# Halo x loads taken at a lower rate in the placement estimate, their work placed with more slack, and a last output tile left whole, in a hybrid attention and pooling layer

## The reference

```python
h = rms_norm(x, norm_gain)
proj = einsum('bsd,de->bse', h, w_in)      # 2048 -> 16384 columns
q, k, v, z_attn, u_pool, z_pool, gates = split(proj)
# A: three dilated sliding windows (128,1) (512,4) (2048,16), 8 heads each, mixed by softmax denominators
y_attn = (attn * silu(z_attn)) @ w_branch_attn
# B: trailing means over 2, 4, 8, 16 positions minus the token, 256 channels each
pool = concat(d_g @ pool_maps[g]) * pool_scale
y_pool = (pool * silu(z_pool)) @ w_branch_pool
g_attn, g_pool = split(sigmoid(gates + b_gates))
out = x + (g_attn * y_attn + g_pool * y_pool) @ w_out
```

## Time and profile before

| | |
|---|---|
| median of 3 runs | 1585.2 us |
| the profiled run | 1585.16 us, span of its slowest core (core 4) 1583.4 us |
| spans of the cores 0 to 7 | 1579.7, 1579.3, 1581.5, 1577.0, 1583.4, 1577.5, 1580.2, 1579.9 us |
| core 4: TensorE busy | 1545.1 us, 98% of the span |
| core 4: VectorE, ScalarE busy | 639.8 us (40%), 602.3 us (38%) |
| core 4, 80 to 120 us: TensorE busy, granted clock, DMA share | 35.60 of 40 us, 0.91, 0.97 |
| core 4, 120 to 160 us | 38.98 of 40 us, 1.00, 0.89 |
| core 4, 160 to 200 us | 38.72 of 40 us, 1.00, 0.43 |
| core 4, 200 to 1500 us | 1298.1 of 1300 us, 1.00 |

### The profile page before, as it was taken

How to read it: one execution, slowest core, us unless ns; L and a number is a source line. 1 busy time by engine, 2 the same in 40 slices (tenths; PEclk the granted TensorE clock), 3 DMA queues, 4 the chain that set the end, 5 groups by cost and what they waited for, 6 DMA issues and landing times.

```text
span 1583.4 us, 27047 instructions; the slowest of 8 cores (1577.0 to 1583.4 us)
## 1 busy us (share of the span) xinstructions
PE 1545.1 (98%) x10216; PEld 935.8 (59%) x10216; DVE 639.8 (40%) x840; ACT 602.3 (38%) x985; POOL 86.9 (5%) x168
## 2 busy tenths in 40 slices
PE   5889999999999999999999999999999999999997
PEld 4655668656864756849656964856544444444443
DVE  5777723165415445543164515354522211113211
ACT  3667535353435543455353435553631111110000
POOL 0000000000000000000000000000000101000000
PEclk8999999999999999999999999999999999999999
DMA  9798441123131143231123131243545556542983
GB/s 241 186 246 216 90 84 33 27 52 73 31 54 34 35 78 68 48 68 32 35 54 64 32 54 34 50 72 63 120 81 92 97 105 107 89 73 39 207 218 107
DMA packets 43073, 138.04 MB, mean 87 GB/s; under 512 B 7041, under 2 KB 8321, under 8 KB 39681
## 3 DMA queue, kind: packets, MB, share of 16 engines
q0 software_dynamic: 23552, 85.58, 32.1%
q1 hardware_dynamic: 14640, 42.29, 8.4%
q10 hardware_dynamic: 4754, 8.45, 1.9%
HBM read 206.86 MB, written 10.49 MB: 137 GB/s over the span
## 4 chain that ended last, share of the span: by engine, by line
PE 90%; DMA 4%; DVE 2%; ACT 2%; issue 1%; SPq 0%; DVEq 0%; ACTq 0%
PE p_pp L464 74%; PE p_pnd L464 6%; PE p_psc L464 5%; PE p_pS L464 3%; DMA s_xt<-xh 3%; DMA pt_spill<-s_pt 1%; DVE s_ub L475 1%; ACT s_xn L545 1%; PE p_pnd L568 1%; ACT s_rr L468 1%; DVE s_xn L479 0%; DMA s_rot<-s_qS 0%; DMA s_rot<-s_kS 0%; ACT s_jk L545 0%; DVE s_kS L475 0%
## 5 line engine op out<-in xcount | busy, mean ns | idle before, releaser
L464 PE MATMUL p_pp<-s_hTo,s_wr 128*128 128x512 bf16 (+4 forms) x3616 | 765.1, 365 | 10.4 <-DMA s_wr<-w_in 4.4
L464 PEld LDWEIGHTS p_pp<-s_hTo,s_wr 128*128 128x128 bf16 x3616 | 343.1, 99 | 368.0 <-issue 16.2
L479 DVE SCALAR_TENSOR_TENSOR s_kS<-p_pp,s_cst,s_rr 128x512 bf16<-128x512 f32 (+1 forms) x96 | 94.6, 986 | 271.1 <-ACT s_rr L468 236.6
L464 PE MATMUL p_pp<-s_wr,s_hTo 128*128 128x256 bf16 x1536 | 175.4, 273 | 1.4 <-DVE s_qS L479 1.4
L464 PEld LDWEIGHTS p_pp<-s_wr,s_hTo 128*128 128x128 bf16 x1536 | 160.7, 119 | 8.0 <-issue 1.7
L464 PE MATMUL p_pp<-s_wr,s_hTh 128*128 128x256 bf16 x1344 | 159.5, 273 | 0.0
L464 PE MATMUL p_pp<-s_hTh,s_wr 128*128 128x512 bf16 (+1 forms) x768 | 155.2, 352 | 0.0
L468 ACT ACTIVATE s_rr<-p_pS 128x512 f32<-128x512 f32 x144 | 83.6, 580 | 181.8 <-PE p_pS L464 172.9
L464 PEld LDWEIGHTS p_pp<-s_wr,s_hTh 128*128 128x128 bf16 x1344 | 145.3, 137 | 1.9
L468 ACT ACTIVATE s_rr<-s_rr 128x512 f32<-128x512 f32 x208 | 128.5, 618 | 19.7 <-ACT s_rr L468 1.1
L487 POOL DMA_DIRECT2D s_wr<-w_in x128 | 67.7, 529 | 1212.1 <-PE p_pp L464 760.9
(11 more groups left out here) (75 smaller groups left out, 1203.8 us busy)
## 6 DMA issues: line engine op xcount, KB each, us to landing
s_wr<-w_in POOLq DMA_DIRECT2D x128, 512.0 KB, 5.1
s_xt<-xh SPq DMA_DIRECT2D x23, 1024.0 KB, 9.4
s_wr<-w_y POOLq DMA_DIRECT2D x16, 512.0 KB, 4.9
s_wo<-w_out POOLq DMA_DIRECT2D x16, 512.0 KB, 7.4
s_xr<-xh ACTq DMA_DIRECT2D x32, 256.0 KB, 7.5
out<-s_ob SPq DMA_DIRECT2D x31, 256.0 KB, 6.0
pt_spill<-s_pt SPq DMA_DIRECT2D x8, 256.0 KB, 6.5
s_pT<-pt_spill SPq DMA_DIRECT2D x1, 2048.0 KB, 12.3
```

The costliest lines, as they stand in the source:

```text
L464: S.op("pe", lambda t: t.matmul(out, lhsT=lhsT, rhs=rhs, start=start, stop=stop), reads=reads, writes=writes, cost=n / 2400.0 + 0.0025)
L479: S.op("dve", lambda v: v.scalar_tensor_tensor(out=out, in0=in0, scalar=scalar, in1=in1, op0=op0, op1=op1), reads=reads, writes=writes, co ...
```

## The change

Three edits. The first: a DMA of 1 MB or more on SyncE's queue is taken to move 180 KB per us in the planner's estimate, where it was 270. The second: the margin of a condition is now its own field, 0.6 us as before except for the two conditions of a halo tile (its Square and scale, and each half of its transposes), where it is 2.5 us. Both act through the planner alone: the same instructions, in other places of the lists. The third: the last of the 32 output tiles, which was done as two halves of 256 columns, each with its own matmuls, addition and DMA, is done like the others.

```diff
         if o.isdma:
             self.T[eng] = at + 0.1
-            self.chan[eng] = max(self.chan[eng], at + 1.5) + kb / (270.0 if kb >= 1024 else 540.0)
+            rate = 180.0 if eng == "sp" else 270.0
+            self.chan[eng] = max(self.chan[eng], at + 1.5) + kb / (rate if kb >= 1024 else 540.0)
             o.end = self.chan[eng] + 0.7
...
     def when(self, t):
         c = t.cond
-        at = self.S.ready_at(c.reads, c.writes) + self.MARGIN
+        at = self.S.ready_at(c.reads, c.writes) + c.margin
         for r in c.rings:
             i = r.ctr % r.n
-            at = max(at, self.S.ready_at((), (r.B[i],)) + self.MARGIN)
+            at = max(at, self.S.ready_at((), (r.B[i],)) + 0.6)
...
-                yield Cond(reads=[xt.B[loaded[j]]], rings=[xn], heavy=XLATE)
+                yield Cond(reads=[xt.B[loaded[j]]], rings=[xn], heavy=XLATE, margin=2.5)
...
-                    yield Cond(reads=[xn.B[slot[j]], B_id], rings=[pnd], heavy=XLATE)
+                    yield Cond(reads=[xn.B[slot[j]], B_id], rings=[pnd], heavy=XLATE, margin=2.5)
...
-                parts = [(0, 512)] if (cg, tt_) != (3, 7) else [(0, 256), (256, 256)]
-                for part, (c0, cn) in enumerate(parts):
-                    if part:
-                        P, BP = banks[n_out % 4]
-                    for db in range(KC):
-                        mm(P[:, c0:c0 + cn], mT[:, db, ts_], wo[cg][:, db, c0:c0 + cn], db == 0, db == KC - 1, cn,
-                           [B_mT[db], B_wo[cg]], [BP])
-                    o_ap = ob_t[oi][:, c0:c0 + cn]
-                    stt(o_ap, P[:, c0:c0 + cn], 0.5, xr_t[xi][:, c0:c0 + cn], ALU.mult, ALU.add, cn, [BP, xr.B[xi]],
-                        [ob.B[oi]])
-                    cs = slice(512 * cg + c0, 512 * cg + c0 + cn)
-                    S.op("sp", lambda s, o_ap=o_ap, ts_=ts_, cs=cs: s.dma_start(out=out_d[ts_, cs], in_=o_ap),
-                         reads=[ob.B[oi]], dsem="dp2" if part else f"do{oi}", kb=cn // 2)
+                for db in range(KC):
+                    mm(P[:], mT[:, db, ts_], wo[cg][:, db, :], db == 0, db == KC - 1, 512, [B_mT[db], B_wo[cg]], [BP])
+                stt(ob_t[oi][:], P[:], 0.5, xr_t[xi][:], ALU.mult, ALU.add, 512, [BP, xr.B[xi]], [ob.B[oi]])
+                S.op("sp", lambda s, oi=oi, ts_=ts_, cs=cs: s.dma_start(out=out_d[ts_, cs], in_=ob_t[oi][:]),
+                     reads=[ob.B[oi]], dsem=f"do{oi}", kb=256)
```

More of the change, by code:

```diff
@@ L207, with __init__ @@
 class Cond:
-    __slots__ = ("reads", "writes", "rings", "after", "heavy")
-    def __init__(self, reads=(), writes=(), rings=(), after=(), heavy=0.0):
+    __slots__ = ("reads", "writes", "rings", "after", "heavy", "margin")
+    def __init__(self, reads=(), writes=(), rings=(), after=(), heavy=0.0, margin=0.6):
         self.heavy = heavy
+        self.margin = margin
         self.reads = reads
@@ L225 @@
 class Tasks:
-    MARGIN = 0.6
     def __init__(self, S):
```

## The result

The changed kernel took 1589.97 us in the median of seven runs, the kernel before 1584.89 in the runs beside them: a ratio of 1.0036 with a 95% interval of 1.0023 to 1.0048, or 3.6 to 7.6 us slower. The profiled run took 1589.7 us. The forecast was 1589.1 us and slower. The spans of the cores 0 to 7 are 1581.5, 1583.3, 1588.1, 1586.4, 1586.3, 1583.7, 1585.2 and 1581.5 us: all are longer than before, by 1.6 to 9.4 us. The slowest core is now core 2; I compare core 4 with itself, and then add what core 2 has more.

What follows compares the result with a forecast made beforehand. TensorE, busy for 98% of the span, was taken as the bound. On 1585.16 us, -7.2 + 3.6 + 5.4 + 0.1 = +1.9 gives 1587.1, and 2.0 for the clock 1589.1 us; range 1584.5 to 1591.5.

Steps and rivals of the forecast that it cites:

- gaps of tiles 13 and 14, half clock: Pooling stage, core 4: TensorE's waits before these tiles' transposes and the half clock behind them go, -7.2 us together.
- tile 9 behind the `s_zs` wait: First group: tile 9's transposes, which ran ahead of the wait at 77.46, now stand behind it, +0.9 us.
- z3's map, z1's bank: First group: z3's map waits for the bank of z1's map, given back behind tile 14's scale, +0.7 us.
- second u group, z3's bank: First group: the second u group waits for z3's bank, given back by z3's product behind tile 15's scale, +1.9 us.
- second group: z4 waits 0.4 us for z1's product and the second u group 0.84 where it waited 1.18: +0.1 us.
- fourth group: The wait of 1.28 us there stays, its ends being tile 20's transposes and an unchanged ScalarE and VectorE chain: 0.
- tile 23: End of pooling stage: its Square now stands behind tile 22's copy and z3's silu, so TensorE waits, +5.4 us, every core.
- clock behind it: TensorE's clock falls to half behind the new wait before tile 23, costing between 0 and 2.5 us, taken as +2.0.
- last tile: Kernel's end: the last output tile done whole lands at 1578.4 instead of 1578.3 us, +0.1, bounds -0.3 and +0.4.
- rival 1: The clock holds behind the new wait before tile 23: 1587.1 us, within 0.2%; chance 0.20.
- rival 4: More falls of the clock, also at the 1.9 us wait in the first group: 1591.6 us; chance 0.09.
- Rival 2: Loads land earlier and the first group's bank waits don't come, -2.6: 1584.5 us without a clock fall; chance 0.13.

Runs made afterwards that it cites:

- The filled wait: Changed kernel with 24 matmuls of 512 columns, result unused, put before tile 23's transposes: 1587.36 us, ratio 1.0023 to the kernel before.
- tile 23 repaired: Changed kernel with tile 23's Square and scale placed as soon as tile 21 is transposed: 1581.68 us, ratio 0.9989 to the kernel before.
- the halves with one buffer: Changed kernel with tile 23's Square early, a semaphore per spill buffer, and the last tile again in two halves sharing one output buffer: 1578.75 us, ratio 0.9963.
- the last tile alone: Kernel before with the last output tile whole and the new rate, margin kept at 0.6: 1583.17 us, ratio 0.9993 to the kernel before.

## Why the prediction was right, step by step

The time, the sign and the main step came out as forecast. The size of the change did so less well: +3.9 us were forecast, and the ratio gives 5.7. Core 4 of the two profiled runs, start to start:

| step | forecast | measured |
|---|---|---|
| gaps of tiles 13 and 14, half clock | -7.2 | gone, all three |
| tile 9 behind the `s_zs` wait | +0.9 | 1.57 for 0.65 in the bracket: +0.9 |
| z3's map, z1's bank | +0.7 | 0.53 + 0.16: +0.7 |
| second u group, z3's bank | +1.9 | 2.48 + 0.16: +2.6 (0 to 4.2 on other cores) |
| second group | +0.1 | 1.04 + 0.77 for 1.18: +0.6 |
| fourth group | 0 | 1.44 for 1.28: +0.2 |
| tile 23 | +5.4 | 5.20 + 0.16: +5.4 on all cores |
| clock behind it | +2.0 | +2.35 |
| last tile | +0.1 | -1.1 |

The fourth group's 1.44 is that of six other cores; core 4's bracket there is 1.65 before a row of 3 matmuls, since the record of one is missing. Without the last tile the rows give +5.6, the marks +5.2 (from the end of the `s_zs` wait, 77.46 and 78.12, to the third projection, 198.87 and 204.71), against a forecast of +3.8; 0.4 of the rows is not accounted for. Core 4 then won back 1.9 us, as the run before had 1.8 us of the attention units' waits in it and this one 0.2. The sentence that no later gap takes in the loss was right for the mean and loose for one core: 0.66 + 5.18 - 1.86 - 1.08 = 2.9 is what core 4's span grew by (the start of the stage, the stage, the attention units, the last tile), and the slowest core's grew by 1588.1 - 1583.4 = 4.7.

**Tile 23: right, and shown three ways.** A sum of six durations over three engines (8.45 - 3.05) gave 5.4, and 5.36 came. No DMA is in the chain, and the eight cores agree to 0.01 us, where the waits that end with a load differ by microseconds.

**The clock: right, low by a third of a microsecond.** The fall came on all eight cores, at 1.9 to 2.7 us, so rival 1 falls. The filled wait isolates its price.

**The bank waits: right in kind, wrong in size.** The step that failed is that z3's product would run at 116.1. It did so at 117.09 on core 4, because tile 15's load came for a Square at 112.13, where the earlier trace rows had 110.76; on core 2 it was 112.90. I had read one core and used its landing time as fixed. Over the cores the wait was 0 to 4.17, and the slowest core is the one where it was longest and the clock fell twice (on core 3 it fell twice too). That is rival 4's mechanism, on a core that I hadn't looked at. Rival 2 happened on cores 0 and 7, where the wait is absent; it could not help, since the time is the slowest core's.

**The gain was overdrawn for the kernel as a whole.** -7.2 holds for core 4. Before, cores 1, 2, 6 and 7 had a gap of the same size before tile 14 (3.62 to 4.20 us, clock 0.50 to 0.66 from 110 to 115 us), but cores 3 and 5 had 1.62 and 0.94 us, and core 0 kept its clock. With tile 23 repaired the two planner edits are worth 0.6 to 1.5 us, not 3.6.

**The last tile: wrong in sign, and outside its bounds of -0.3 and +0.4.** The addition ended 4.62 us after the first matmul, near the forecast (4.7 to the DMA's start), and 5.10 before: -0.48, as the sum had it. Two steps failed. The first is the length of the DMAs: the second half's was to take "as the first, 1.9" and took 2.8 on core 4, and the whole tile's was to take 2.5 and took 3.1, so that the landing came 0.2 us earlier and not 0.1 later. The second is a term that the sum put at nothing without saying so: it ended with the landing, and from there to the end of the span were 4.2 us before and 3.3 after. That is 0.9 of the 1.1 us. The planner's edits were forecast 1.4 too low and the last tile 1.2 too high on core 4, and these nearly cancelled. Core 4's attention units took 1.9 us less in this run by chance, and another core was the slowest. So part of the closeness of 1589.1 is luck.

The Trainium skill's rule ("DMA: Bandwidth & Descriptors", "Anatomy of one DMA") would have given -0.7 for the last tile, as an estimate (-0.6 when I redo the sum). The measured -1.1 is nearer to it than to my +0.1, but that is no support for it: 0.9 of it lies behind the landing, which the rule does not cover, and on core 4 before one DMA of 128 KB took 1.9 and the next 2.8, where the rule has 2.3 for both.

## What to carry to other kernels

When a planner's slack is raised, look first at the last item of each stage: every item before it can be put off at little cost, but behind the last one the engine has nothing to do, and the chain of its producers stands open. Where a wait ends with a DMA, read its landing on every core before putting a number on it; the time is set by the core where it is worst. A repair of one wait is worth what the next wait in line leaves of it. And an end of a kernel is summed up to the end of the span, not to the last landing: what the engines still wait through behind it was worth more here than the whole question of halves or not.

## What the runs showed of the hardware

A wait of 5.20 us was followed by half clock on eight of eight cores, at a price of 1.9 to 2.7 us (2.35 on core 4). Shorter ones went either way, and not by their length alone: 4.17 and 2.80 us (cores 2 and 3 of after) and 2.44 (core 3 of the kernel with the wait filled) with a fall, 2.48 (core 4 of after) and 3.57 (core 0 of before) without. 24 matmuls of no use in the wait kept the clock at 2.4 GHz on all eight cores.

The last output DMA, from issue to landing, took 2.5 to 3.0 us for 128 KB over the cores of before and 1.8 to 2.4 over those of the halves with one buffer; for 256 KB it took 3.0 to 3.2 in after and 2.3 to 3.3 with the last tile alone. From the landing to the end of the span were 4.17, 3.51 or 3.31 us where the last DMA raises `dp2`, `do0` or `do3`. The waits that the engines still have behind that semaphore (16, 3, none) fit this; it is not shown by a run that changes nothing else.

A 1 MB load on SyncE's queue took 13.74 us on one core and 16.43 on another of the same execution, and landed 0.8 us later there.
